# Hybrid decoder step on Trainium2: the last two experts run as one merged pass

## What is computed

```
h = xblk @ w_up[e] + b_up[e]
glu, lin = h[:, :D_FF], h[:, D_FF:]
glu = jnp.minimum(glu, SWIGLU_LIMIT)
lin = jnp.clip(lin, -SWIGLU_LIMIT, SWIGLU_LIMIT)
act = glu * jax.nn.sigmoid(SWIGLU_ALPHA * glu) * (lin + 1.0)
yb  = act @ w_down[e] + b_down[e]
y   = sum over the token's 4 experts of gate * yb
out = layer_norm(ALPHA * x + y, ln2_g, ln2_b)
```

## Time and profile before

| | |
|---|---|
| median of 3 runs (lowest to highest) | 1234.68 us (1234.62 to 1236.22) |
| the profiled execution: its time | 1238.43 us |
| the profiled execution: its span | 1236.6 us |
| TensorE busy, of the span | 1205.2 us (97%) |
| VectorE (DVE), ScalarE (ACT) busy | 374.3 us (30%), 197.3 us (16%) |
| mean granted TensorE clock | 0.994 |
| bytes moved, mean rate | 452.10 MB, 366 GB/s |
| shares of the chain that ended last | TensorE 76%, DMA 23%, DVE 1% |

### The profile page before, as it was taken

How to read it: one execution, slowest core, us unless ns; L and a number is a source line. 1 busy time by engine, 2 the same in 40 slices (tenths; PEclk the granted TensorE clock), 3 DMA queues, 4 the chain that set the end, 5 groups by cost and what they waited for, 6 DMA issues and landing times.

```text
span 1236.6 us, 14913 instructions
## 1 busy us (share of the span) xinstructions
PE 1205.2 (97%) x6419; PEld 582.3 (47%) x6419; DVE 374.3 (30%) x843; ACT 197.3 (16%) x425; POOL 4.6 (0%) x12
## 2 busy tenths in 40 slices
PE   9999999999999999999999999999999999999996
PEld 8888888867333333333333333333333333333332
DVE  1467076135322222222222232222222222222223
ACT  1244372001111000011111000110110110000002
POOL 0000000000000000000000000000000000000000
PEclk9999999999899999999999999999999999999999
DMA  9722455973899999999999999999999999999994
GB/s 366 249 100 90 170 205 185 321 277 139 306 421 430 430 432 429 428 431 431 429 430 431 430 430 430 430 430 431 431 430 428 431 431 430 430 431 431 429 429 181
DMA packets 55121, 452.10 MB, mean 366 GB/s; under 512 B 5792, under 2 KB 24512, under 8 KB 27000
## 3 DMA queue, kind: packets, MB, share of 16 engines
q1 hardware_dynamic: 54352, 448.70, 87.6%
q0 software_dynamic: 272, 1.37, 0.3%
q10 hardware_dynamic: 432, 1.08, 0.2%
HBM read 449.70 MB, written 2.54 MB: 366 GB/s over the span
## 4 chain that ended last, share of the span: by engine, by line
PE 76%; DMA 23%; DVE 1%; issue 0%; ACT 0%; SPq 0%; DVEq 0%
PE pair L1218 24%; PE pair L1263 14%; PE pair L957 13%; DMA slots<-in_w_up 12%; DMA raw<-in_w_up 10%; PE pair L1024 5%; PE pair L1165 4%; PE pair L1291 3%; PE pair L1179 1%; PE pair L1206 1%; PE pair L1248 1%; PE pair L1043 1%; PE pair L1050 1%; PE pair L1194 1%; PE pair L952 1%; PE pair L934 1%
## 5 line engine op out<-in xcount | busy, mean ns | idle before, releaser
L1218 PE MATMUL pair<-slots,xg 128*64 128x512 f32 x1424 | 320.5, 595 | 10.3 <-DMA slots<-in_w_up 10.0
L1218 PEld LDWEIGHTS pair<-slots,xg 128*64 128x64 f32 x1424 | 98.4, 137 | 211.6 <-issue 186.8
L1774 DVE TENSOR_TENSOR xT<-xT,pair 128x528 f32<-128x528 f32 x120 | 76.5, 698 | 396.6 <-PE pair L1291 396.6
L1263 PE MATMUL pair<-slots,at 128*64 128x512 f32 x736 | 167.9, 598 | 0.8 <-ACT at L823 0.8
L957 PE MATMUL pair<-xT,raw 128*128 128x264 f32 x704 | 159.6, 386 | 0.0
L1218 PE MATMUL pair<-raw,xg 128*64 128x512 f32 x624 | 141.1, 595 | 9.1 <-DMA raw<-in_w_up 9.1
L957 PEld LDWEIGHTS pair<-xT,raw 128*128 128x128 f32 x704 | 132.7, 190 | 22.7 <-issue 0.4
L819 ACT ACTIVATE sig<-gsb 128x512 f32<-128x512 f32 x32 | 20.2, 630 | 465.9 <-DVE gsb L1784 465.9
L1263 PEld LDWEIGHTS pair<-slots,at 128*64 128x64 f32 x736 | 48.9, 136 | 92.5 <-issue 80.3
L1218 PEld LDWEIGHTS pair<-raw,xg 128*64 128x64 f32 x624 | 43.1, 137 | 97.8 <-issue 80.3
L1291 PE MATMUL pair<-gt,ysb 64*128 64x264 f32 x496 | 69.4, 409 | 0.0
(11 more groups left out here) (302 smaller groups left out, 834.3 us busy)
## 6 DMA issues: line engine op xcount, KB each, us to landing
slots<-in_w_up SPq DMA_DIRECT2D x89, 2048.0 KB, 28.6
slots<-in_w_down SPq DMA_DIRECT2D x44, 2048.0 KB, 33.1
raw<-in_w_up SPq DMA_DIRECT2D x39, 2048.0 KB, 34.8
raw<-in_w_down SPq DMA_DIRECT2D x18, 2048.0 KB, 37.0
raw<-in_w_tiled SPq DMA_DIRECT2D x22, 1024.0 KB, 5.3
raw<-in_w_rnn_out SPq DMA_DIRECT2D x8, 640.0 KB, 11.6
raw<-in_w_attn_out SPq DMA_DIRECT2D x4, 1024.0 KB, 5.1
raw<-in_w_out_tiled SPq DMA_DIRECT2D x4, 1024.0 KB, 4.7
```

The costliest lines, as they stand in the source:

```text
L1218: last = pe.matmul(to[h * CAP:(h + 1) * CAP, :], xg[:, 2 * (i % 2) + row, i // 2, :], w[:, c:c + 512], start=False, stop=i == UPP - 1 and ...
L1263: last = pe.matmul(DOWN[h * CAP:(h + 1) * CAP, :], at[:, kk, i - UPP, :], w[:, kk * D + h * 512:kk * D + (h + 1) * 512], start=i == UPP an ...
L1774: ins = dve.tensor_tensor(y, y, more, ALU.add)
```

## The change

The last two experts, 30 ("A") and 31 ("B"), leave the loop and the closing block and become one pass written by hand: A's four up pairs, B's four up pairs, A's two down pairs, B's two down pairs. The written-out blocks are now 29 (`NSTAT`), so the loop runs expert 29. The last four pairs of the new order are A's and B's down pairs; three of them are read in pieces (`END_PARTS`), each piece with its own semaphore. A's output no longer goes through `combine` and DVE's additions: it is added to the closing accumulators like B's, with A's gates from `gt` and B's from `gnew`. B's down projection has its own accumulator (`LIN`) and its own turned activation (`at_b`, in the memory of `gx`).

```
-NSTAT = 30
+NSTAT = 29
...
-LAST_PARTS = ((0, 2), (2, 3), (3, 4))
+END_A, END_B = NE - 2, NE - 1
+END_PAIRS = [(END_A, i) for i in range(4)] + [(END_B, i) for i in range(4)] + [(END_A, 4), (END_A, 5), (END_B, 4), (END_B, 5)]
+END_PARTS = {9: ((0, 2), (2, 4)), 10: ((0, 2), (2, 4)), 11: ((0, 2), (2, 3), (3, 4))}
...
+        at_b = gx[:, :].rearrange("p (j h n) -> p j h n", j=4, h=2)
...
+            def end_pair(blk, j, i, row0):
...
+                to, src = down_parts(dst, i, row0)
+                for (k0, k1), done in zip(END_PARTS.get(j, ((0, 4),)), end_part.get(j, [landed])):
+                    sp.dma_start(to[:, k0:k1, :], src[:, k0:k1, :]).then_inc(done, 16)
...
-            sigmoid(end)
+            sigmoid(end_a)
+            take_act(end_a)
+            take_gather(end_b)
+            take_turned(end_b)
+            sigmoid(end_b)
             act.activation(warm[:, :], warm[:, :], ACT.Sqrt)
-            take_act(end)
-            take_y(end)
+            take_act(end_b, at_b)
+            take_y(end_a, 2 * UPP + 2)
+            take_y(end_a, 2 * PER, LIN)
...
+            def down_end(j, to, source):
...
+                for p, (k0, k1) in enumerate(END_PARTS.get(j, ((0, 4),))):
+                    if j in END_PARTS:
+                        pe.wait_ge(end_part[j][p], 16)
+                    else:
+                        landed(end_a, j)
+                    for kk in range(k0, k1):
+                        for h in range(2):
+                            last = pe.matmul(to[h * CAP:(h + 1) * CAP, :], source[:, kk, j % 2, :],
...
-            up(end, 0)
-            combine(end)
-            up(end, 1)
-            pe.wait_ge(added, count(end, 4, 0))
+            up(end_a, 0)
+            up(end_a, 1)
+            combine(end_a)
+            up_end(end_a)
+            pe.wait_ge(added, count(end_a, 4, 0))
+            gather(end_b)
...
+            turn_act(end_a)
+            biases_and_samples()
+            routes()
+            turn_gathered(end_b)
+            pe.wait_ge(xg_ready, count(end_b, 1, 1))
+            up(end_b, 0)
             presum(0)
-            up_end(end)
-            pe.wait_ge(glu_taken, count(end, 1, 1))
+            up(end_b, 1)
+            pe.wait_ge(gnew_ready, count(end_b, 1, 1))
             presum(1)
+            up_end(end_b)
+            pe.wait_ge(at_ready, count(end_a, 1, 1))
+            down_end(8, DOWN, at)
+            pe.wait_ge(glu_taken, count(end_b, 1, 1))
             presum_quarters()
-            turn_act(end)
-            pe.wait_ge(at_ready, count(end, 1, 1))
-            down(end, UPP)
-            down(end, UPP + 1)
-            pe.wait_ge(y_ready, count(end, 1, 1))
-            pe.wait_ge(gt_ready, count(end, 1, 1))
-            last_block(0)
-            last_block(1)
-            last_quarters()
+            turn_act(end_b)
+            down_end(9, DOWN, at)
+            pe.wait_ge(y_ready, count(end_a, 1, 1))
+            pe.wait_ge(gt_ready, count(end_a, 1, 1))
+            last_block(0, gt, False)
+            last_block(1, gt, False)
+            last_quarters(gt, False)
+            pe.wait_ge(at_ready, count(end_b, 1, 1))
+            pe.wait_ge(lin_taken, count(end_b, 1, 1))
+            down_end(10, LIN, at_b)
+            down_end(11, LIN, at_b)
+            pe.wait_ge(y_ready, count(end_b, 1, 1))
+            last_block(0, gnew, True)
+            last_block(1, gnew, True)
+            last_quarters(gnew, True)
...
-            end = Blk(NSTAT, n, True)
-            adds(end)
-            copy_gates(end)
-            activate(end)
+            end_a, end_b = Blk(NSTAT, n, True), Blk(NSTAT + 1, n, True)
+            run(end_a, C_LAST + 1)
+            activate(end_b, count(end_a, PER, 2 * UPP))
```

More of the change, by code:

```diff
@@ L288, in build @@
         LN2_PAIR = 2
[L289 removed]
+        ln2 = ring[(LOOP_PAIR + PER + LN2_PAIR) % NP]
         def rows_of(t):
@@ L439, in build @@
         Blk = namedtuple("Blk", "first k last")
-        LOOP_PAIR = NSTAT * PER
+        in_loop = [q % NP for q in range(LOOP_PAIR, LOOP_PAIR + PER)]
         def after(blk):
@@ L609, in _ @@
                     expert_pair(Blk(NSTAT, k, False), i, row0)
-            for i in range(PER):
-                q = LOOP_PAIR + PER + i
+            for j, (expert, i) in enumerate(END_PAIRS):
+                q = LOOP_PAIR + PER + j
                 if q < LOOP_PAIR + NP:
@@ L1253, in down @@
                 w, _, _ = place(blk, i)
-                final = blk.last and i == PER - 1
-                if not final:
-                    landed(blk, i)
+                landed(blk, i)
                 if blk.first == 1 and i == NP - PER:
@@ L1365, in presum_quarters, with last_block @@
                                   start=k == 0, stop=False)
-            def last_block(t):
+            def last_block(t, gates, final):
                 t0, _ = TILES[t]
                 for h in range(2):
[L1371 to L1375, removed]
+                    last = pe.matmul(pair[FINAL[t]][:, h, :], gates[h * CAP:(h + 1) * CAP, t0:t0 + P],
+                                     ysb[h * CAP:(h + 1) * CAP, :], start=False, stop=final)
+                if final:
+                    last.then_inc(final_done, 1)
@@ L1377, in last_quarters @@
+            def last_quarters(gates, final):
                 for q in (0, 2, 1, 3):
                     r, c = slice(q // 2 * CAP, q // 2 * CAP + CAP), q % 2 * QUARTER
[L1379 to L1385 removed]
@@ L1386, in _ @@
-            combine(end)
-            up(end, 1)
-            pe.wait_ge(added, count(end, 4, 0))
+                    last = pe.matmul(QUARTERS[32 * q:32 * q + 32, :], gates[r, T - 32:T], ysb[r, c:c + QUARTER],
+                                     start=False, stop=final)
+                if final:
+                    last.then_inc(final_done, 1)
+            def down_end(j, to, source):
+                w, _, _ = place(end_a, j)
+                for p, (k0, k1) in enumerate(END_PARTS.get(j, ((0, 4),))):
[6 more added lines that the diff above has]
+                            last = pe.matmul(to[h * CAP:(h + 1) * CAP, :], source[:, kk, j % 2, :],
+                                             w[:, kk * D + h * 512:kk * D + (h + 1) * 512],
+                                             start=j % 2 == 0 and kk == 0, stop=j % 2 == 1 and kk == 3)
+                last.then_inc(used_up, 1)
```

62 lines of the change are left out of this document (31 added, 31 removed).

## The result

The changed kernel took 1240.22 us (median of 6 runs, 1237.1 to 1241.29), the kernel before 1234.97 us (6 runs, 1234.62 to 1238.72) beside it. The ratio is 1.0027, with a 95% interval from 1.0014 to 1.0040: slower by 1.7 to 4.9 us. The forecast was +1.9 us and a median of 1236.6; the median measured lies 1.2 us above the top of the range. The rest lies ahead of the experts: a stage there takes longer in some executions than in others, whichever kernel it is, and the two kernels drew unevenly, as the repeated runs show.

What follows compares the result with a forecast made beforehand. After A3 lands, TensorE's own queue was taken to bound the end. +1.58 + 0.39 + 0.67 - 0.75 = +1.9 us (bounds +1.35 to +2.15) gave a median of 1236.6 us, 8-in-10 range 1234.4 to 1239.0.

Steps and rivals of the forecast that it cites:

- What bounds the end: After A3 lands at 1178.86, TensorE's own queue of work and two gaps (0.75 and 0.67 us) set the end.
- The landings: Weight pairs after A3 land when the nth did before: A4 at 1203.3, B5 by 1220.8; smallest margin about 4 us.
- The gather: Before B's up matmuls, nothing covers ACT's two copies around the turning of B's gathered tokens: +1.58 us, at most 1.8.
- A's contribution: A's output goes straight into the closing accumulators, 2.56 us, instead of through the combine matmuls, 2.17 us: +0.39 us.
- The second wait: After A5's matmuls TensorE waits for ACT to copy A's output, with B4 queued behind: +0.67 us.
- The gap that goes: Before B's down matmuls, ACT's copy of B's activation is covered by A4's and A5's matmuls: -0.75 us.
- The pieces at nothing: Last four pairs go out as eight transfers instead of six; TensorE waits for none, so zero effect.
- From the profiled execution to the median: Whole program: profiled 1238.43 us becomes 1240.3; being 3.75 us above the median 1234.68, the median forecast is 1236.6.
- The clock did not fall in the gather: Rival: granted clock falls in B's uncovered gather, around 1189, losing 5.1 us, time 1241.7; chance 0.08.
- The pieces did not slow the stream: Rival: two more transfers delay the last landing to 1229.2, TensorE loses 4.3 us, time 1240.9; chance 0.03.
- The stream does not bind: Rival: the weight stream binds between A3 and B3, so less loss (1236.0) or a gain; chance 0.10, real gain 0.05.
- the change did what it says: Rival: the gather's gap is filled or A's wait hidden by something unseen; time stays 1234.7; chance 0.05.

## Why the prediction was right or wrong, step by step

- **What bounds the end: right.** TensorE's own queue and its gaps, not the stream: no matmul of any run waited for a pair after A3.
- **The landings: right.** A4, issued at 1161.35, landed 41.9 us later at 1203.3, the predicted figure. B5's last piece, issued at 1187.5, landed 30.8 us later at 1218.3, ahead of the 1220.8 given as its latest.
- **The gather, +1.58: it was +1.51.** By the chain B0's matmuls start 10.18 us after A3's landing. Before, the work ahead of A4 took 1186.85 - 1178.86 = 7.99 us and the turning 0.68; 10.18 - 7.99 - 0.68 = 1.51. Both gaps came as described; the first hand-over to TensorE took 0.04 us and not 0.12.
- **A's contribution, +0.39: +0.38.** A's closing additions last from 1216.28 to 1218.83, 2.55 us, against 2.17.
- **The second wait, +0.67: +0.67** (1215.61 to 1216.28), and shown by taking it away (-0.77).
- **The gap that goes, -0.75: right**, and got back in the old order too (-0.78).
- **The sum, +1.9: +1.85.** From A3's landing to the end of B5's matmuls 47.0 was predicted; 1225.88 - 1178.91 = 46.97. (The upper bound, +2.15, adds up to 2.14.) What follows B5 takes 12.62 us in both.
- **The pieces at nothing: right inside the span.** Outside it some 0.3 us were missed, by time less span; the times themselves do not show them.
- **From the profiled execution to the median: wrong.** "It is 3.75 us above the median, 1234.68, so the forecast for the median is 1236.6" took that offset as the runs' own scatter. For the profiled execution the forecast was 1240.3, and 1240.7 was measured. But two of the three times behind it, 1234.62 and 1234.68, are such as executions have whose clock holds in the routing stage, about a quarter of all, while the earlier trace rows showed that the profiled one was of the others. So 1236.6 is a forecast for the high group, where 1236.75 was measured, and 1240.3 one for the low group, where the median was 1240.09. A median of either group can come up, 3.2 us apart, so "the runs' own spread", which I took as 1.6 us, was half of what it should have been. With it the range would have had to reach 1240. That the first measurement put most of before in one group and most of the changed kernel in the other was luck of the draw.
- **The chances.** By the first ratio, 1.0027, it was slower by more than 0.2%, to which I had given 0.30; in the three comparisons of the merged order that differ from it in pieces at most, the ratio was 1.0015 to 1.0018 (+1.9 to +2.2 us), just inside 0.2%, where the forecast lay.
- **The rivals.** The clock did not fall in the gather (1.00 from 1185 to 1200). The 5.1 us that I gave for such a fall were too many by what the routing stage shows: 10.2 us at half speed put the experts off by 3.7. The pieces did not slow the stream: the last landed 39.4 us after A3, and read whole 39.3, so the cost for each added transfer that the prediction sets against the margin did not add up here. The stream does not bind, and the change did what it says.

## What to carry to other kernels

A merge that puts two dependent chains side by side saves the waits it covers and exposes those that the old interleaving covered; count the copies between engines on both sides, at some 0.7 us each here, before anything else. A gap of that kind can be closed by moving a piece of independent work behind the instruction that triggers the copy; here that won 0.78 us in the old order, by the trace, without a merge. And before a sum is set against a median, look whether the profiled execution and the median are of the same kind: a stretch in which the granted clock differs between executions makes groups, and a few runs may show only one of them.

## What the runs showed of the hardware

- The same program runs the routing stage with a granted clock of 1.00 in about a quarter of its executions (62 of 233, by the mean clock), and in the others, as far as profiled, at 0.50 for 6.8 to 6.9 or for 10.2 us; the longer fall moves the experts by 3.7 us, and the medians of the two groups are 3.2 apart. Before the fall TensorE was busy for all but 0.15 us from 292 to 306 in either kind of execution, at a clock of 1.00; its rows there do not tell which way an execution will go, and the cause was not found.
- Time outside the span differs between kernels by some 0.3 us (1.77 to 1.88 in the kernel before, 1.81 to 2.28 in the merged ones with seven pieces), so a difference of spans is not yet one of times.
- A gap of 0.69 to 0.77 us between TensorE and ACT, once covered, gave back 0.77 to 0.78 us of the stretch from A3's landing to the close: all of it, and no other wait took its place while the work used as a cover was not wanted elsewhere. Moved from a place where it was wanted, it opened a wait of 0.95 us there.
